# The sample tile of a fused input projection in fp32 on four column groups, and the projection slices moved between two units

## The chip, the cores and the metric

The kernel runs on one core of a Trainium2 chip. The metric is the device time of one execution in microseconds (us), as the median of several runs. The engines are TensorE (PE; its weight loads are shown apart as PEld), VectorE (DVE), ScalarE (ACT), GpSimd (POOL) and SyncE (SP), which here only starts DMAs.

## What is computed

Two layers of a transformer step over 512 prompt tokens and 32 sample tokens of width 1024. Layer 0 (the even one) mixes four differential-attention heads with eight stick-breaking heads; layer 1 (the odd one, "fox") is forgetting attention with 16 heads. In both, normed tokens are first projected by one wide weight; after the attention come an output projection and a mixture of experts. Cut to what the change touches:

```
x = concat(x_prompt (512 rows), x_sample (32 rows))
h = rmsnorm(x) * (1 + scale) + shift            # scale, shift from adaLN, apart for prompt and sample
q, k, v = split(h @ w_in)                       # w_in: 1024 x 3072, in fp32
# prompt rows attend to prompt rows; sample rows attend to 256 cached rows and to the 32 sample rows
# k and v of all rows are outputs as well
```

## The kernel before

A layer's projection and attention run together, as a pipeline over eight **blocks** of weight columns (NB = 8). A block is 384 columns (BW): 128 each of q, k and v, so one differential head or two of the other heads. The tokens stand in five **tiles**: t = 0 to 3 are 128 prompt rows each, t = 4 (called NT) is the 32 sample rows. A **unit** u = 5 i + t is the attention of block i for query tile t.

For each block, `fuse_load` (SP) brings the raw fp32 weights into `fu_raw`, in two halves of four DMAs. `fuse_high` (ACT, L612) rounds them to the fast format fp32r, `fuse_low` (DVE, L618) makes the rest, in four pieces. The tokens h are held in the same way, transposed, as `hT` and `hT2`. A **product** is one tile by one block: eight **slices** (one for each 128 of the 1024 inputs), and a slice is three matmuls (L563, L564, L565) of 128 rows by 384 columns: high by high, high by low, low by high. It goes into bank 0 or 1, alternately. The sample's tile takes the same 24 matmuls, as 128 columns of `hT` are loaded from its first column on, and only 32 of the 128 result rows are kept. The results are copied to `fu_rows` by `fuse_rows_act` (ACT, even t, L661) and `fuse_rows_dve` (DVE, odd t, L668).

The order on each engine is written out by hand. On PE, in `even_pe` and `fox_pe`, unit u holds: the scores of unit u+1 (`first` or `scores`), the transposes of its own weights (`second` or `turn`), the values (`values`), and between them slices of the product that is six units ahead, n = u + 6. In units 0 to 3 these are slices 0 to 2 (or 4), then up to 6, then 6 and 7. In unit 4 PE also transposes q and k of the next block (`turn_q_k`, L676) and its late keys (`turn_rest`, L676); the slices stand there in pairs. Unit 3 of block i so holds the sample's product of block i+1, and unit 4 the first product of block i+2. Before unit 0 comes a **lead** (`lead_pe`): it transposes h (L526), makes all five products of block 0 and the first of block 1. In layer 1 the lead also has `gate_logits` (matmuls on `wf_r`), whose results pass through a chain on DVE and ACT (L1691 to L1599) to the first scores. Other work on PE between the units: `ada_matvec` (L326), a vector by 512 columns in fp32 on four groups of 32 array columns, and `ada_sum` (L332).

On ACT, `q_out` (L1560) and `late_out` (L1564, L1565) bring the transposes of unit 4 out; then ACT copies tile 0 (L661), takes the exponentials of unit 0 (L1539) and copies the transposed weights (L1550). On DVE, `maxima` (L1630) and `normed` (L1637, L1640) do their part; `k_out` is L1647, `mixed` is L1654. Layer 0 has the same with other lines (values L942 for stick-breaking). SP starts in layer 1, for each block, the stores of k and v (`store`), then `fuse_load` of the block two ahead, then adaLN loads.

## Time and profile before

| what | value |
|---|---|
| median of 3 runs | 1740.81 us (1735.86 to 1748.72) |
| the profiled execution | 1750.45 us, of which the span is 1748.7 us |
| PE busy | 1486.2 us, 85% of the span |
| DVE, ACT, POOL busy | 1032.4, 865.5, 489.7 us |
| mean granted TensorE clock | 0.924 of full speed |
| bytes read from HBM | 341.87 MB |

The span is the time between the first and the last instruction; the time of the execution has 1.75 us around it. Busy time of PE adds up matmuls that overlap in its pipeline, so what a matmul costs is read from the distance of starts, not from its own length.

### The profile page before, as it was taken

To read this page: it belongs to the slowest core of one execution; us is meant where nothing else is said; L and a number is where in the kernel's file an instruction comes from. 1 tells how busy PE (TensorE), PEld (TensorE's weight loads), DVE (VectorE), ACT (ScalarE), POOL (GpSimd) and SP (SyncE) were. 2 spreads that over 40 slices of the span, in tenths; PEclk is the share of its full clock that TensorE was granted. 3 is DMA by queue.
4 is the path that set the end of the run, shared out by engine and by line. 5 is a ranking of instruction groups with operands and counts; after the bars stand their busy time and mean duration, and the time that the engine had idled before them with its cause. 6 is when DMAs were issued, how large, how long until landed. Compare 5 with 4: busy or idle time off the path is not lost.

```text
span 1748.7 us, 22798 instructions
## 1 busy us (share of the span) xinstructions
PE 1486.2 (85%) x7979; PEld 1162.0 (66%) x7979; DVE 1032.4 (59%) x1345; ACT 865.5 (49%) x1512; POOL 489.7 (28%) x379
## 2 busy tenths in 40 slices
PE   3499999997947999999937899999889399999981
PEld 0387777764735777877727677777567277878770
DVE  0555442224446988988956443333363568888995
ACT  2233334445124777777733333333341267788772
POOL 1200111110104666656521000000001155656650
PEclk8699999998967999999968999999989599999995
DMA  8435553133044899989970333443420479999984
GB/s 279 147 120 180 187 170 104 68 124 106 1 195 154 337 351 356 369 342 354 357 249 12 98 104 104 129 136 114 155 75 36 167 263 344 367 367 364 335 314 170
DMA packets 148608, 358.62 MB, mean 205 GB/s; under 512 B 18660, under 2 KB 80868, under 8 KB 122420
## 3 DMA queue, kind: packets, MB, share of 16 engines
q1 hardware_dynamic: 136184, 333.25, 52.7%
q0 software_dynamic: 12352, 24.40, 3.8%
q8 instruction: 45, 0.74, 0.2%
q14 instruction: 27, 0.22, 0.0%
HBM read 341.87 MB, written 33.56 MB: 215 GB/s over the span
## 4 chain that ended last, share of the span: by engine, by line
PE 65%; DVE 12%; issue 7%; ACT 6%; DMA 5%; SPq 2%; DVEq 1%; POOL 0%; POOLq 0%; ACTq 0%; PEldq 0%; PEld 0%
PE bank L563 17%; PE bank L565 15%; PE bank L564 15%; DVE ring_r L1945 4%; DMA ring<-in_w_gate 2%; PE bank L326 2%; ACT work_r L1938 2%; PE bank L1447 2%; PE bank L1485 1%; PE bank L676 1%; PE bank L332 1%; PE bank L1462 1%; PE bank L2231 1%; PE bank L919 1%; PE bank L558 1%
## 5 line engine op out<-in xcount | busy, mean ns | idle before, releaser
L564 PE MATMUL bank<-ring_r,arena_r 128*128 128x512 f32 x816 | 323.6, 397 | 0.0
L563 PE MATMUL bank<-ring_r,hT_r 128*128 128x384 f32 x640 | 239.9, 375 | 1.6 <-ACT hT_r L494 1.6
L564 PE MATMUL bank<-ring_r,hT_r 128*128 128x384 f32 x640 | 217.0, 339 | 0.0
L565 PE MATMUL bank<-ring_r,work_r 128*128 128x384 f32 x640 | 217.0, 339 | 0.0
L1945 DVE TENSOR_TENSOR ring_r<-ring,work_r 128x1024 fp32r<-128x1024 f32 x102 | 177.2, 1763 | 28.2 <-ACT work_r L1938 28.2
L1945 DVE TENSOR_TENSOR ring_r<-ring,arena_r 128x1024 fp32r<-128x1024 f32 x96 | 166.4, 1771 | 29.3 <-ACT arena_r L1938 29.3
L564 PEld LDWEIGHTS bank<-ring_r,arena_r 128*128 128x128 f32 x816 | 157.3, 193 | 31.1
L1945 DVE TENSOR_TENSOR ring_r<-ring,hT_r 128x1024 fp32r<-128x1024 f32 x108 | 155.1, 1464 | 25.1 <-ACT hT_r L1938 24.3
L1938 ACT ACTIVATE hT_r<-ring 128x1024 fp32r<-128x1024 f32 x144 | 144.3, 1054 | 47.3 <-DMA ring<-in_w_gate 41.5
L563 PEld LDWEIGHTS bank<-ring_r,hT_r 128*128 128x128 f32 x640 | 121.7, 190 | 43.0 <-issue 39.1
L1938 ACT ACTIVATE work_r<-ring 128x1024 fp32r<-128x1024 f32 x136 | 136.6, 1059 | 6.9 <-DMA ring<-in_w_up 6.8
L1938 ACT ACTIVATE arena_r<-ring 128x1024 fp32r<-128x1024 f32 x128 | 126.8, 1052 | 21.6 <-DMA ring<-in_w_down 21.3
L1889 POOL TENSOR_TENSOR arena<-arena,bc 128x1024 f32<-128x1024 f32 (+1 forms) x6 | 14.3, 2382 | 434.9 <-DVE arena L1875 434.9
L563 PE MATMUL bank<-hT_r,arena_r 128*128 128x512 f32 x288 | 123.2, 428 | 8.9 <-DVE arena_r L2386 5.6
L564 PEld LDWEIGHTS bank<-ring_r,hT_r 128*128 128x128 f32 x640 | 122.2, 191 | 1.2 <-issue 0.7
L565 PEld LDWEIGHTS bank<-ring_r,work_r 128*128 128x128 f32 x640 | 121.3, 190 | 0.0
L565 PE MATMUL bank<-hT_r,arena_r 128*128 128x512 f32 x288 | 118.4, 411 | 0.0
L2421 POOL TENSOR_TENSOR ring_r<-ring,arena_r 128x1024 fp32r<-128x1024 f32 x32 | 86.3, 2696 | 90.9 <-ACT arena_r L1938 90.9
L563 PE MATMUL bank<-work_r,arena_r 128*128 128x512 f32 x272 | 109.2, 402 | 0.0
L2421 POOL TENSOR_TENSOR ring_r<-ring,hT_r 128x1024 fp32r<-128x1024 f32 x36 | 92.4, 2566 | 54.0 <-ACT hT_r L1938 40.4
L563 PE MATMUL bank<-arena_r 128*128 128x512 f32 x256 | 100.9, 394 | 6.7 <-DVE ring_r L1945 6.6
L565 PE MATMUL bank<-work_r,arena_r 128*128 128x512 f32 x272 | 106.4, 391 | 0.0
(356 smaller groups left out, 2880.3 us busy)
## 6 DMA issues: line engine op xcount, KB each, us to landing
ring<-in_w_gate SPq DMA_DIRECT2D x68, 1024.0 KB, 6.8
ring<-in_w_up SPq DMA_DIRECT2D x68, 1024.0 KB, 7.4
ring<-in_w_down SPq DMA_DIRECT2D x68, 1024.0 KB, 7.5
bc<-in_w_ada SPq DMA_DIRECT2D x40, 1024.0 KB, 6.8
bc<-in_w_in_even SPq DMA_DIRECT2D x64, 192.0 KB, 4.0
bc<-in_w_in_odd SPq DMA_DIRECT2D x64, 192.0 KB, 3.6
ring<-in_w_ada SPq DMA_DIRECT2D x4, 2048.0 KB, 12.3
arena<-moe_out SPq DMA_DIRECT2D x8, 1024.0 KB
```

The source lines that it names most:

```text
L326: last = nc.tensor.matmul(acc[32 * q:32 * q + 32, :], silu_c[:, 4 * h + q, :], ada_w[h][:, q, :], start=h == 0, stop=h == 1)
L332: nc.tensor.matmul(acc[0:32, :], pick[:, :], ada_part(pre), start=True, stop=True).then_inc(AD["sum"], 1)
L558: last = nc.tensor.matmul(acc, wr[:, k, :], hT[:, k, cols(t)], start=k == 0, stop=k == KD - 1)
L563: nc.tensor.matmul(acc, rows_hi, w_hi, start=first, stop=False)
L564: nc.tensor.matmul(acc, rows_hi, w_lo, start=False, stop=False)
L565: return nc.tensor.matmul(acc, rows_lo, w_hi, start=False, stop=last)
L676: last = nc.tensor.transpose(out_bank[0:np_, c:c + r], src, ident[0:r, 0:r])
L919: last = nc.tensor.matmul(b[:, 0:n], neg_from[:, :], s[:, 0:n], start=False, stop=True, skip_group_check=True)
L1447: nc.tensor.matmul(fx_bank(u, h)[0:r, 0:n], fx_qT[i % 2][half, cols(t)], fx_kT[i % 2][half, k0:k0 + n], start=True, stop=False)
L1938: act.activation(r32(piece(m_high[v], q)), piece(m_low[v], q), ACT.Copy).then_inc(MO[f"hi_{c}"], 1)
L1945: dve.tensor_tensor(r32(piece(m_low[v], q)), piece(m_low[v], q), f32(piece(m_high[v], q)), ALU.subtract).then_inc(MO[f"lo_{c}"], 1)
L2421: pool.tensor_tensor(r32(piece(m_low[v], 1)), piece(m_low[v], 1), f32(piece(m_high[v], 1)), ALU.subtract).then_inc(MO[f"lop_{c}"], 1)
```

## The change

1. The sample's product is no longer 24 fp32r matmuls. DVE copies the sample's transposed rows once for each layer into `sample_T` (`row_sample`), in plain fp32. `fuse_sample` multiplies them with the raw weights of a block: for each of eight slices four matmuls, one for each group of 32 array columns, which take 96 (SW) of the 384 weight columns each. That is 32 matmuls in fp32, each issued as two. ACT copies the result out in four pieces (`sample_rows`).
2. The order on PE. In the blocks, the sample's product is that of block i+2 (before: i+1), all of it in unit 3 between the scores and the transposes; the second stretch of slices in unit 3 is now slices 0 to 3 of the first product of block i+2, and unit 4 keeps slices 4 to 7 of it (1, 2 and 1). In the lead, the sample of block 0 comes ahead of tile 0, into bank 6, and that of block 1 behind tile 3. `gate_logits` in layer 1 is ahead of tile 3 (before: behind it).
3. Waits: `fuse_load` of block b also waits for the sample's product of block b-1, which reads `fu_raw`. The lead waits for `sample_T`. A product into the bank of the sample waits for the four copies. The stores of k and v wait for `ev_s` in place of the third ACT copy.
4. In layer 1's lead on DVE, the copy of tile 3 is later (behind all of `fuse_low` of block 1) and `k_out(0)` is moved from ahead of the chain of the gate to behind it.
5. The matrix `upto` (one memset and one select on POOL in the setup) is gone.

```diff
+        def row_sample(dve, l):
+            s, o = NORM, 2 * l
+            for half in range(2):
+                dve.wait_ge(s["ev_a"], EV_A[o] + half + 1)
+                dve.tensor_copy(sample_T[:, 4 * half:4 * half + 4, :], row_turned(0, half)).then_inc(s["smp"], 1)
...
             row_turn(pe, l, 0)
             row_turn(pe, l, 1)
+            pe.wait_ge(NORM["smp"], 2 * l + 2)
             row_turn(pe, l, 2)
-            for t in range(TILES):
-                row_evicted(pe, l, min(t + 1, TILES - 1))
-                if t == NT:
-                    pe.wait_ge(NORM["pad"], 2 * l + 2)
-                    if last_logits:
-                        last_logits()
+            fuse_sample(pe, l, 0, bank[6], 0, KD)
+            for t in range(NT):
+                row_evicted(pe, l, t + 1)
+                if t == NT - 1 and last_logits:
+                    last_logits()
                 fuse_product(pe, l, t, 0, KD)
                 if t + 3 < TILES:
                     row_turn(pe, l, t + 3)
+            fuse_product(pe, l, NT, 0, KD)
...
             if b >= 1:
                 sp.wait_ge(FU["lo"], 4 * g_b)
+                sp.wait_ge(FU["smp"], g_b)
...
+            b, t = n // TILES, n % TILES
+            if b + t // NT >= NB:
                 return
-            b, t = n // TILES, n % TILES
+            if k0 == 0 and n >= 2:
+                fuse_rows_out(pe, l, n - 2)
+            if t == NT:
+                fuse_sample(pe, l, b + 1, bank[n % 2], k0, k1)
+                return
...
+        def fuse_sample(pe, l, b, acc, k0, k1):
+
+            w = by_row(fu_raw)
+            for k in range(k0, k1):
+                if k % 4 == 0:
+                    pe.wait_ge(FU[f"raw{k // 4}"], 64 * (NB * l + b) + 64)
+                for q in range(4):
+                    last = nc.tensor.matmul(acc[DEC * q:DEC * (q + 1), 0:SW], sample_T[:, k, :], w[:, k, SW * q:SW * (q + 1)],
+                                            start=k == 0, stop=k == KD - 1)
+            if k1 == KD:
+                last.then_inc(FU["smp"], 1)
...
+        def sample_rows(act, l, b, acc):
+
+            act.wait_ge(FU["smp"], NB * l + b + 1)
+            fuse_rows_free(act, l, b)
+            for q in range(4):
+                act.activation(fu_rows[b % 2][0:DEC, NT, SW * q:SW * (q + 1)], acc[DEC * q:DEC * (q + 1), 0:SW],
+                               ACT.Copy).then_inc(FU["ev_s"], 1)
...
                 if t == NT:
-                    fuse_product(pe, 1, n, 0, 2)
                     if i + 1 < NB:
                         turn_q_k(i + 1)
                     turn(u)
-                    fuse_product(pe, 1, n, 2, 4)
+                    fuse_product(pe, 1, n, 4, 5)
                     if i + 1 < NB:
                         turn_rest(i + 1)
-                    fuse_product(pe, 1, n, 4, 6)
+                    fuse_product(pe, 1, n, 5, 7)
                     values(u)
                     if i + 1 < NB:
                         scores(u + 1)
-                    fuse_product(pe, 1, n, 6, KD)
+                    fuse_product(pe, 1, n, 7, KD)
                 else:
                     scores(u + 1)
                     k = 4 if t == 0 else 2
-                    fuse_product(pe, 1, n, 0, k)
+                    if t == NT - 1:
+                        fuse_product(pe, 1, n, 0, KD)
+                    else:
+                        fuse_product(pe, 1, n, 0, k)
                     turn(u)
...
-                    fuse_product(pe, 1, n, k, 6)
+                    if t == NT - 1:
+                        fuse_product(pe, 1, n + 1, 0, 4)
+                    else:
+                        fuse_product(pe, 1, n, k, 6)
                     values(u)
...
-                    fuse_product(pe, 1, n, 6, KD)
+                    if t < NT - 1:
+                        fuse_product(pe, 1, n, 6, KD)
...
+                if t == 0 and 1 <= i < NB - 1:
+                    sample_rows(act, 1, i + 1, sample_bank(i + 1))
                 fuse_rows_act(act, 1, u + TILES)
...
-            k_out(0)
+            fuse_rows_dve(dve, 1, 3)
             dve.wait_ge(FG["act"], FG_ACT["log"])
...
             dve.drain().then_inc(FG["dve"], 1)
+            k_out(0)
             maxima(0)
```

PE in units 3 and 4 of a block of layer 1, before (L1447, L1451 and L1453 are the scores, L1462 the transposes, L1485 the values, L676 `turn_q_k` and `turn_rest`; of each stretch of slices the last row stands):

```order
L1447 MATMUL bank<-arena 32x288 x2
...
L565 MATMUL bank<-ring_r,work_r 128x384
L1462 MATMUL bank<-ident,arena 128x128 x8
...
L565 MATMUL bank<-ring_r,work_r 128x384
L1485 MATMUL bank<-arena 64x128 x8
...
L565 MATMUL bank<-ring_r,work_r 128x384
L676 MATMUL bank<-ident,arena 128x128 x8
L1462 MATMUL bank<-ident,arena 128x32 x2
```

The same place after the change (the lines are those of the changed kernel: L1496 the scores, L1511 the transposes, L1534 the values, L717 `turn_q_k`, L652 the sample, L569 the third matmul of a slice):

```order
L1496 MATMUL bank<-arena 32x288 x2
L1500 MATMUL bank<-d_b,sel_b 32x288 x2
L1502 MATMUL bank<-causal_b,ident_b 32x32 x2
L652 MATMUL bank<-bc,sample_T 32x96 x32
L1511 MATMUL bank<-ident,arena 128x128 x8
...
L569 MATMUL bank<-ring_r,work_r 128x384
L1534 MATMUL bank<-arena 64x128 x8
L717 MATMUL bank<-ident,arena 128x128 x8
L1511 MATMUL bank<-ident,arena 128x32 x2
```

The stretch of slices behind the scores has become the 32 matmuls of the sample, and none stands any longer between the values of unit 3 and `turn_q_k`.

ACT between unit 4 of one block of layer 1 and unit 0 of the next, before:

```order
L1564 ACTIVATE arena<-bank 128x288
L1565 ACTIVATE arena<-bank 128x32
L661 ACTIVATE arena<-bank 128x384
L1539 ACTIVATE arena,small<-bank,small 128x128 x2
L612 ACTIVATE ring_r<-bc 128x768
```

and after:

```order
L1619 ACTIVATE arena<-bank 128x288
L1620 ACTIVATE arena<-bank 128x32
L679 ACTIVATE arena<-bank 32x96 x4
L699 ACTIVATE arena<-bank 128x384
L1594 ACTIVATE arena,small<-bank,small 128x128 x2
L618 ACTIVATE ring_r<-bc 128x768
```

The sample's four copies stand ahead of the copy of tile 0 and of the exponentials of unit 0; before, one copy of 32x384 (L661) stood ahead of `q_out`.

DVE in layer 1's lead, around the chain of the gate, before:

```order
L668 COPY arena<-bank 128x384
L1683 TENSOR_SCALAR arena<-bank,bf_t 16x512
L1684 TENSOR_SCALAR arena<-bank,bf_t 16x32
L1686 COPY arena<-bank 16x256
L618 TENSOR_TENSOR ring_r<-bc,ring_r 128x768 x2
L1647 COPY arena<-bank 128x512
L1691 SCALAR_TENSOR_TENSOR arena<-arena 16x544
```

and after:

```order
L1741 TENSOR_SCALAR arena<-bank,bf_t 16x512
L1742 TENSOR_SCALAR arena<-bank,bf_t 16x32
L1744 COPY arena<-bank 16x256
L624 TENSOR_TENSOR ring_r<-bc,ring_r 128x768 x2
L706 COPY arena<-bank 128x384
L1749 SCALAR_TENSOR_TENSOR arena<-arena 16x544
```

The copy of tile 3 now stands ahead of L1749 (before: L1691), and `k_out(0)` (L1647) no longer does.

## Rows read from the trace of the kernel before

**Rows 1.** Windows of one block each, layers 0 and 1: us, busy times, clock, DMA

```profile
148.60:186.92 38.32, 38.32 (x239) 29.09 (x243) 19.56 (x53) 13.65 (x39) 4.08 (x6) 1.00 0.52 174
281.07:325.49 44.42, 44.37 (x266) 32.70 (x270) 12.08 (x21) 20.71 (x54) 7.32 (x11) 1.00 0.32 103
1072.40:1111.36 38.96, 38.96 (x273) 29.99 (x276) 15.07 (x35) 14.77 (x43) 0.00 (x0) 1.00 0.36 113
```

**Rows 2.** Timeline of PE, units 3 and 4 in layer 1: start, us

```profile
1084.15 0.45 PE L563 MATMUL bank<-ring_r,hT_r 128*128 128x384 f32 x1
...
1085.32 1.04 PE L1462 MATMUL bank<-ident,arena 128*128 128x128 f32 x8
...
1087.26 0.45 PE L563 MATMUL bank<-ring_r,hT_r 128*128 128x384 f32 x1
...
1089.56 1.09 PE L1485 MATMUL bank<-arena 128*64 128x128 f32 x16
1090.58 0.44 PE L563 MATMUL bank<-ring_r,hT_r 128*128 128x384 f32 x1
...
1092.80 1.03 PE L676 MATMUL bank<-ident,arena 128*128 128x128 f32 x8
...
1097.13 0.66 PE L1485 MATMUL bank<-arena 128*64 128x32 f32 x12
...
1099.57 0.70 PE L1447 MATMUL bank<-arena 64*128 64x256 f32 x4
...
1102.70 0.38 PE L1462 MATMUL bank<-ident,arena 128*128 128x128 f32 x2
```

**Rows 3.** Timeline of PEld and PE at one matvec on four column groups

```profile
1072.33 0.16 PEld L326 LDWEIGHTS bank<-bc,silu_c 128*32 128x32 f32 x8 [0.17 <-issue]
1072.79 0.13 PEld L326 LDWEIGHTS bank<-bc,silu_c 128*32 128x32 f32 x4 [0.30 <-issue]
1073.22 0.13 PEld L326 LDWEIGHTS bank<-bc,silu_c 128*32 128x32 f32 x4 [0.30 <-issue]
...
1072.33 1.92 PE L326 MATMUL bank<-bc,silu_c 128*32 128x512 f32 x16
```

**Rows 4.** Timelines of ACT and DVE around unit 0 of that block

```profile
1096.29 0.19 ACT L1565 ACTIVATE arena<-bank 128x32 f32<-128x32 f32 x1
1099.68 0.49 ACT L661 ACTIVATE arena<-bank 128x384 f32<-128x384 f32 x1 [3.19 <-PE bank L565]
...
1101.10 0.48 DVE L1640 TENSOR_SCALAR arena<-arena,small 128x128 f32<-128x128 f32 x2
```

**Rows 5.** Raw weights of layer 1: page part 6 (us to landing), timelines of SP and ACT

```profile
bc<-in_w_in_odd SPq DMA_DIRECT2D x64, 192.0 KB, 3.6
...
948.68 3.03 ACT L612 ACTIVATE ring_r<-bc 128x768 fp32r<-128x768 f32 x4
...
1094.44 4.15 SPq L603 DMA_DIRECT2D bc<-in_w_in_odd  x8
...
1100.75 0.85 ACT L612 ACTIVATE ring_r<-bc 128x768 fp32r<-128x768 f32 x1
```

**Rows 6.** Timeline of PE, lead of layer 0

```profile
71.66 1.97 PE L526 MATMUL bank<-ident,arena 128*128 128x128 f32 x8 [1.65 <-POOL arena L511]
75.24 0.66 PE L563 MATMUL bank<-ring_r,hT_r 128*128 128x384 f32 x1 [1.62 <-ACT hT_r L494]
76.34 0.52 PE L563 MATMUL bank<-ring_r,hT_r 128*128 128x384 f32 x1
```

**Rows 7.** Timelines of DVE and PE, lead of layer 1

```profile
923.20 0.48 DVE L500 TENSOR_TENSOR work_r<-bank,hT_r 128x128 fp32r<-128x128 f32 x2
948.09 0.34 PE L563 MATMUL bank<-ring_r,hT_r 128*128 128x384 f32 x1
952.28 0.40 PE L563 MATMUL bank<-hT_r,wf_r 128*128 128x512 f32 x1
960.56 0.42 PE L563 MATMUL bank<-ring_r,hT_r 128*128 128x384 f32 x1
967.56 0.70 DVE L1691 SCALAR_TENSOR_TENSOR arena<-arena 16x544 f32<-16x544 f32 x1
975.29 0.49 PE L1447 MATMUL bank<-arena 64*128 64x128 f32 x4 [4.21 <-ACT logf L1599]
```

**Rows 8.** Timeline of PE, unit 3 of block 7 in layers 0 and 1

```profile
412.73 1.08 PE L942 MATMUL bank<-arena 128*64 128x512 f32 x4 [0.69 <-ACT arena L1076]
1274.53 1.09 PE L1485 MATMUL bank<-arena 128*64 128x128 f32 x16 [0.85 <-ACT arena L1550]
```

More of the change, by code:

```diff
@@ L224, in setup_pool @@
             pool.affine_select(out=strict_b[:, :], in_=strict_b[:, :], compare_op=ALU.is_ge, fill=NEG, base=-1,
-                               pattern=[[1, P]], channel_multiplier=-1)
-            pool.affine_select(out=upto[:, :], in_=upto[:, :], compare_op=ALU.is_ge, fill=0.0, base=0,
                                pattern=[[1, P]], channel_multiplier=-1)
@@ L429, in encoder_step @@
         junk = arena[:, 14336:15360]
-        NORM = sems("norm", "square", "rstd", "scaled", "shifted", "tr", "ev_a", "ev_v", "self", "gain", "shift_v", "pad")
+        NORM = sems("norm", "square", "rstd", "scaled", "shifted", "tr", "ev_a", "ev_v", "self", "gain", "shift_v", "smp")
         NORM_NO = {"norm_mix0": 0, "norm_ffn0": 1, "norm_mix1": 2, "norm_ffn1": 3}
@@ L628, in fuse_product @@
                     pe.wait_ge(FU["lo"], 4 * (NB * l + b) + k // 2 + 1)
-                if k == 0 and n >= 2:
-                    fuse_rows_out(pe, l, n - 2)
                 last = split_product(bank[n % 2][:, 0:BW], tile_cols(hT_flat, k, t), tile_cols(hT2_flat, k, t),
@@ L657, in fuse_rows_act, with sample_bank @@
             b, t = n // TILES, n % TILES
-            if n < NB * TILES and t % 2 == 0:
-                act.wait_ge(FU["mm"], UNITS * l + n + 1)
+            if n < NB * TILES and t in (0, 2):
+                act.wait_ge(FU["mm"], NT * (NB * l + b) + t + 1)
                 fuse_rows_free(act, l, b)
-                act.activation(fu_rows[b % 2][0:rows(t), t, :], bank[n % 2][0:rows(t), 0:BW], ACT.Copy).then_inc(FU["ev_a"], 1)
+                act.activation(fu_rows[b % 2][:, t, :], bank[n % 2][:, 0:BW], ACT.Copy).then_inc(FU["ev_a"], 1)
         def fuse_rows_dve(dve, l, n):
             b, t = n // TILES, n % TILES
-            if n < NB * TILES and t % 2 == 1:
-                dve.wait_ge(FU["mm"], UNITS * l + n + 1)
+            if n < NB * TILES and t in (1, 3):
+                dve.wait_ge(FU["mm"], NT * (NB * l + b) + t + 1)
                 fuse_rows_free(dve, l, b)
-                dve.tensor_copy(fu_rows[b % 2][0:rows(t), t, :], bank[n % 2][0:rows(t), 0:BW]).then_inc(FU["ev_v"], 1)
+                dve.tensor_copy(fu_rows[b % 2][:, t, :], bank[n % 2][:, 0:BW]).then_inc(FU["ev_v"], 1)
+        def sample_bank(b):
+            return bank[6] if b == 0 else bank[(TILES * b - 1) % 2]
         def fx_bank(u, h):
@@ L1601, in fox_act @@
                 i, t = u // TILES, u % TILES
+                if t == 0 and 1 <= i < NB - 1:
+                    sample_rows(act, 1, i + 1, sample_bank(i + 1))
                 fuse_rows_act(act, 1, u + TILES)
```

78 lines of the change are left out of this document (46 added, 32 removed).

## The prediction

> **What bounds the kernel now.** I read the windows of single blocks first, then the timeline of PE inside one, then what ACT, DVE and SP do beside it. In the blocks of both layers PE is busy for the whole window at clock 1.00, while DVE and ACT are busy for half of it or less [rows 1]. The reader is to see that a block lasts as long as its PE instructions do: what leaves PE there leaves the time, as long as no other engine's chain then ends later. This holds for blocks 0 to 5; in block 7, which has no product beside it, PE waits for ACT and DVE [rows 8], and in the leads it waits for the rows of h [rows 6] and for the gate's chain [rows 7].
>
> **Price of a slice.** Eight slices in a row take 948.09 to 952.28, 4.19 us, so 0.524 us a slice [rows 7]. A short stretch costs more, as PE changes between kinds of matmul: two slices 1084.15 to 1085.32, 1.17 us; four 1087.26 to 1089.56, 2.30 us; the last two of unit 3 with the first two of unit 4 1090.58 to 1092.80, 2.22 us [rows 2]. So each change costs 0.1 to 0.2 us.
>
> **Part 1, the slices that go.** Units 3 and 4 held 16 slices. The 1.17 us behind the scores go, the 2.22 us behind the values of unit 3 go, and of the three pairs left in unit 4 two slices go, 2 x 0.524 = 1.05 us. The four slices at 1087.26 stay, as slices of another product. Sum: 4.44 us of PE in each block.
>
> **Part 2, the sample in fp32.** 32 matmuls, each issued twice, so 64 instructions on four column groups. The trace has this kind with 512 columns: PEld loads weights in groups of four, 1072.79 and 1073.22, so a round of four instructions takes 0.43 us, and all 16 fit into 1.92 us [rows 3]. 96 columns are 96/512 of it: 0.081 us a round, 16 rounds 1.29 us, and 0.25 us for the changes of kind at both ends. I take 1.55 us. The lower bound is 1.29 us. The upper bound comes from the densest short matmuls of the trace, twelve with 32 columns and 64-column weights in 0.66 us [rows 2], of which about 0.22 us is the length of the last: 0.44/11 = 0.04 us an instruction, 64 x 0.04 + 0.25 = 2.8 us. I stay near the lower end because those twelve load twice as many weight columns, and the matvec has the same weights (128x32), the same four groups and the same loop.
>
> **A steady block** so loses 4.44 - 1.55 = 2.9 us. There are six in each layer: 12 x 2.9 = 34.8 us.
>
> **What hides the rest in the steady blocks.** The four copies on ACT stand ahead of the copy of tile 0. ACT is free from the end of L1565, 1096.48, to 1099.68 [rows 4], 3.2 us; a copy is at most the 0.49 us of the 128x384 one, four are at most 1.96 us. The sample's product for them is long done. Slices ahead of that tile-0 copy are one fewer, so copy, exponentials and the transposes that wait for them all come 0.52 us earlier together: the weights are ready at 1101.58 and PE asks at 1102.70 [rows 2, 4], a margin of 1.1 us that stays. In unit 4 the cover is four slices instead of eight, but `turn_q_k` (1.03 us), `turn_rest` and three of the four slices still stand between a transpose and the values that need it, over 2 us for an ACT copy of about 0.5. Bank 0 or 1 is asked for earlier by the first product in unit 3; DVE copies tile 3 out at the start of that unit. The new wait of `fuse_load` ends with the sample's product, early in unit 3, about when `fuse_low` ends, for which it waits anyway. On SP the stores are ahead of it in the queue; they no longer wait for the sample's copy in unit 4, so both should start up to 8 us earlier than 1094.44, for weights that ACT takes at 1100.75 [rows 5]. I cost all of this at nothing; without the cover it is the stall below.
>
> **Layer 0's lead.** It loses the sample's 4.19 us and gains 1.55 us for block 1's. Block 0's sample falls into the 1.62 us in which PE waits for hT [rows 6]. The first slice there takes 1.10 us (75.24 to 76.34), twice 0.524, so the clock is at its lower level, 1.2 GHz, and the sample may last 2.6 us; but what it does slowly the tile behind it then does less slowly. With DVE's two more copies I take 0.2 us. Net 2.4 us.
>
> **Layer 1's lead.** Tile 2 ends at 948.09 [rows 7]; ahead of it come the sample, 1.55 us, and DVE's two copies, below the 0.48 us of the like pair L500, say 0.4. So tile 2 ends near 950.0, the logits (952.28 to 960.56, 8.28 us) near 958.3, tile 3 near 962.5, its copy near 963.2. There the gate's chain starts, which started at 967.56, as `k_out` is out of its way; the first scores come 7.73 us behind that start, so near 970.9 instead of 975.29. PE itself arrived at 971.08 (4.21 us before the scores); it loses 4.19 us and gains twice 1.55 and 0.4: 970.4, and the transposes of the gate's rows still have to pass ACT. I take 971.2, a gain of 4.1 us. The load of block 1 must now wait for block 0's sample, near 936; 4.15 us of issue and 3.6 us to landing make 943.8, and ACT takes it at 948.68 or later [rows 5]. Everything behind the first scores moves with them.
>
> **Block 6.** Its unit 3 held the sample of block 7, now one block earlier: about 1.17 + 2.30 + 1.2 = 4.7 us go with nothing in their place. Bare, the same unit waits 0.69 us in layer 0 and 0.85 us in layer 1 [rows 8]; with the next wait, and a clock that may fall sooner, I take 3.2 us in each layer, between 2.2 and 4.0: 6.4 us.
>
> The setup's two POOL instructions less: nothing, as the setup is not ended by POOL's last select.
>
> **Sum.** 34.8 + 2.4 + 4.1 + 6.4 = 47.7 us. The profiled execution of 1750.45 us would become 1702.8 us. It is 0.6% above the median; against the median of 1740.81 us the same gain gives 1693 us. With 1.44 to 2.1 us for a sample, block 6's bounds and a median that moves by some 6 us (the runs span 1735.86 to 1748.72), this case reaches from 1683 to 1704 us.
>
> **Rivals.**
>
> *Issue-bound sample.* The sample's 128 PE instructions (64 loads, 64 matmuls) have only 0.02 us for each pair. No row shows PE keep that up for 64 of them: the matvec has 16. At the upper bound of 2.8 us each of the 16 samples costs 1.25 us more, 20 us: 1713 us. For it: the count. Against it: in the matvec eight loads start within 0.16 us [rows 3]. The Trainium skill, TensorE: Matmul & The Clock Gate, section "Wait — 56ns, not 53.3ns?", says that starts of matmuls are never closer than about 25 ns, and that the sequencer may spend about 62 ns on each. Sixteen matmuls of about 0.6 us within 1.92 us do not show the first broken or kept; by the second, as an estimate from that page, a sample would take 4.2 us and the kernel 1736 us. By 25 ns it would be 1.85 us and 1698 us, inside my range.
>
> *A stall in the thinned unit.* With four slices fewer in unit 4 one wait ends last: the exponentials of unit 0 behind ACT's four copies. It decides once those copies end over 1.1 us late, against a free stretch of 3.2 us. At 1.5 us for each of 12 blocks, 18 us: 1711 us.
>
> *The column groups run one after another (slower).* Then a sample is 64 x 0.081 + 0.25 = 5.4 us, 3.9 us more than taken, 62 us in all: 14 us above before, 1755 us. It decides where a round of four passes (4.44 - 0.25)/16 = 0.26 us in place of 0.081; from there a steady block gains nothing. Against it stands the matvec: sixteen of its instructions, one after another, would take 6.9 us and took 1.92.
>
> **How the numbers follow.** Forecast 0.68; issue-bound 0.16; stall 0.10; serial groups 0.03; a gain beyond the range 0.03. The predicted time is 1693 us. From 1682 to 1714 us takes in the forecast, and both rivals at their price, and leaves out what lies beyond them. About 1% is what a measurement of this kernel can tell from no change; below 1723 us counts as faster: 0.94. Within 1%, by the serial groups or an issue rate near the slow end: 0.045. Slower by over 1%: 0.015.
>
> **What the changed profile would show.** Blocks 35.4 to 36.1 us apart in layer 1 (38.96 before) and PE still busy throughout; the group of L652 with 64 starts within 1.3 to 1.6 us; no wait of PE longer than 0.3 us in units 3, 4 and 0 of blocks 1 to 5; the first scores of layer 1 some 4 us sooner, with PE's wait ahead of them below 1 us; raw weights issued in unit 3. The forecast is wrong if the sample's stretch passes 2.1 us, if PE waits for ACT ahead of unit 0's transposes, or if ACT's L618 waits for a DMA in the blocks.

## The result, and the profile after

| | median of runs | ratio to before, 95% interval |
|---|---|---|
| before | 1741.49 us (1735.86 to 1748.72, 4 runs) | |
| changed | 1691.21 us (1689.09 to 1696.15, 4 runs) | 0.971 (0.9683 to 0.9737) |

That is 50.3 us less (predicted: 1693 us, 47.7 us less). The profiled execution took 1689.62 us, its span is 1687.9 us, 60.8 us less than the span before. PE's busy time went from 1486.2 to 1431.1 us and is still 85% of the span.

First the windows of one block each, in the order and with the columns of [rows 1]:

```profile
141.52:177.01 35.49, 35.49 (x276) 26.34 (x275) 19.38 (x54) 14.12 (x42) 4.07 (x6) 1.00 0.57 188
266.69:308.22 41.53, 41.49 (x304) 29.93 (x303) 11.98 (x21) 21.18 (x57) 7.28 (x11) 1.00 0.35 109
1035.16:1071.27 36.11, 35.95 (x309) 27.07 (x309) 15.06 (x35) 15.24 (x46) 0.00 (x0) 1.00 0.41 126
```

The columns are the window, its length, the busy time and count of PE, PEld, DVE, ACT and POOL, PE's granted clock, the DMA share and GB/s. The blocks are 2.83, 2.89 and 2.85 us shorter, and PE is still busy for all of them (but for 0.16 us in layer 1) at full clock. The window lost what PE lost, and DVE, the next busiest, is busy for 55% at most.

The timeline of PE in units 3 and 4 of one block of layer 1, which answers to [rows 2]:

```profile
1046.98 1.53 PE L652 MATMUL bank<-bc,sample_T 128*32 128x96 f32 x64
1048.44 1.09 PE L1511 MATMUL bank<-ident,arena 128*128 128x128 f32 x8
1049.46 1.04 PE L329 MATMUL bank<-bc,pick 128*32 128x512 f32 x2
1050.44 0.44 PE L567 MATMUL bank<-ring_r,hT_r 128*128 128x384 f32 x1
...
1052.74 1.09 PE L1534 MATMUL bank<-arena 128*64 128x128 f32 x16
1053.76 1.09 PE L717 MATMUL bank<-ident,arena 128*128 128x128 f32 x8
```

The sample's whole product is the first line: 64 starts, and the transposes begin 1.46 us behind its first (1.55 predicted). The four moved slices stand from 1050.44 to 1052.74, 2.30 us, as the slices in this place did before. No line in this stretch has idle time in brackets.

The lead of layer 1 answers to [rows 7]. Its first transposes before, then the timeline of PE after; L1496 here is the first scores, L1534 the first values:

```profile
918.62 1.03 PE L526 MATMUL bank<-ident,arena 32*128 32x32 f32 x8 [27.52 <-POOL arena L511]
```

```profile
890.12 1.03 PE L529 MATMUL bank<-ident,arena 32*128 32x32 f32 x8 [27.51 <-POOL arena L514]
902.94 1.94 PE L529 MATMUL bank<-ident,arena 128*128 128x128 f32 x8 [6.14 <-issue]
904.81 2.75 PE L652 MATMUL bank<-bc,sample_T 128*32 128x96 f32 x64
907.50 0.44 PE L567 MATMUL bank<-ring_r,hT_r 128*128 128x384 f32 x1
...
942.89 0.49 PE L1496 MATMUL bank<-arena 64*128 64x128 f32 x4 [0.49 <-issue]
...
953.37 0.70 PE L1534 MATMUL bank<-arena 128*64 128x128 f32 x4 [5.16 <-ACT arena L1605]
```

From the first transpose to the first scores it is 52.77 us; before it was 56.67 (918.62 to 975.29, the latter in [rows 7]). The wait ahead of the scores was 4.21 us and is 0.49 us. The sample of block 0 runs here at the lower clock level (granted 0.50; 2.75 us in place of 1.53).

By stages, from the starts of the adaLN matvecs, which both kernels have at the same places: up to the last matvec of layer 0, 23.3 us less (406.08 and 382.79); layer 1 from its first transposes to its first matvec 3.0 less (75.81 and 72.83); its six steady blocks 17.1 less (233.72 and 216.64); its block 6 4.8 less (32.44 and 27.66). That is 48.1 us (the terms are rounded). The other 12.7 us between the two profiles lie in the two stages of experts with the output projections, where the kernels do not differ: 512.5 against 507.3 us in layer 0, 488.1 against 480.6 in layer 1. In the profile of e4, which has the old code there as well, these took 506.4 and 491.2 us. So they vary by some us from execution to execution, and the medians, 50.3 us apart, agree with the 48.1 of the stages.

### The profile page after: what moved, and what is told of

Its sections match the earlier page's. It is cut to its first block, busy times and chain, and to the rows that moved or that the text cites. A ratio compares the mean times of both kernels' runs of the same rounds, so it can differ in the third digit from the quotient of the medians.

```text
span 1687.9 us, 24152 instructions
## 1 busy us (share of the span) xinstructions
PE 1431.1 (85%) x8611; PEld 1110.8 (66%) x8619; DVE 1010.1 (60%) x1349; ACT 874.6 (52%) x1560; POOL 495.2 (29%) x377
## 4 chain that ended last, share of the span: by engine, by line
PE 65%; DVE 10%; DMA 8%; issue 6%; ACT 6%; SPq 2%; DVEq 1%; POOLq 0%; ACTq 0%; PEldq 0%; POOL 0%; PEld 0%
PE bank L567 15%; PE bank L569 14%; PE bank L568 14%; DMA ring<-in_w_gate 4%; DVE ring_r L2004 3%; PE bank L323 2%; DMA ring<-in_w_down 2%; PE bank L1496 2%; PE bank L1534 2%; ACT work_r L1997 1%; PE bank L652 1%; PE bank L717 1%; PE bank L1511 1%; PE bank L329 1%; PE bank L959 1%
## 5 line engine op out<-in xcount | busy, mean ns | idle before, releaser
L2004 DVE TENSOR_TENSOR ring_r<-ring,work_r 128x1024 fp32r<-128x1024 f32 x102 | 173.5, 1726 | 33.1 <-ACT work_r L1997 33.0
L567 PE MATMUL bank<-ring_r,hT_r 128*128 128x384 f32 x512 | 191.8, 375 | 0.0
L2004 DVE TENSOR_TENSOR ring_r<-ring,arena_r 128x1024 fp32r<-128x1024 f32 x96 | 157.6, 1676 | 30.6 <-ACT arena_r L1997 30.6
L569 PE MATMUL bank<-ring_r,work_r 128*128 128x384 f32 x512 | 172.8, 337 | 0.0
L568 PE MATMUL bank<-ring_r,hT_r 128*128 128x384 f32 x512 | 172.7, 337 | 0.0
L2004 DVE TENSOR_TENSOR ring_r<-ring,hT_r 128x1024 fp32r<-128x1024 f32 x108 | 144.9, 1369 | 27.0 <-ACT hT_r L1997 25.6
L567 PE MATMUL bank<-hT_r,arena_r 128*128 128x512 f32 x288 | 121.3, 421 | 10.3 <-DVE arena_r L2445 7.1
L569 PE MATMUL bank<-hT_r,arena_r 128*128 128x512 f32 x288 | 117.1, 406 | 0.0
L567 PEld LDWEIGHTS bank<-ring_r,hT_r 128*128 128x128 f32 x512 | 96.6, 189 | 30.2 <-issue 28.1
L2480 POOL TENSOR_TENSOR ring_r<-ring,arena_r 128x1024 fp32r<-128x1024 f32 x32 | 90.7, 2836 | 82.2 <-ACT arena_r L1997 82.2
L569 PE MATMUL bank<-work_r,arena_r 128*128 128x512 f32 x272 | 106.4, 391 | 0.0
L567 PE MATMUL bank<-arena_r 128*128 128x512 f32 x256 | 100.7, 394 | 4.5 <-DVE ring_r L2004 4.0
L569 PE MATMUL bank<-arena_r 128*128 128x512 f32 x256 | 99.8, 390 | 0.0
L568 PEld LDWEIGHTS bank<-ring_r,hT_r 128*128 128x128 f32 x512 | 97.0, 190 | 1.1 <-issue 0.7
```

The lines of the kernel that those rows point to most:

```text
L567: nc.tensor.matmul(acc, rows_hi, w_hi, start=first, stop=False)
L568: nc.tensor.matmul(acc, rows_hi, w_lo, start=False, stop=False)
L569: return nc.tensor.matmul(acc, rows_lo, w_hi, start=False, stop=last)
L2004: dve.tensor_tensor(r32(piece(m_low[v], q)), piece(m_low[v], q), f32(piece(m_high[v], q)), ALU.subtract).then_inc(MO[f"lo_{c}"], 1)
L2480: pool.tensor_tensor(r32(piece(m_low[v], 1)), piece(m_low[v], 1), f32(piece(m_high[v], 1)), ALU.subtract).then_inc(MO[f"lop_{c}"], 1)
```

## The experiments

The medians come from several sessions, in which that of the kernel before lay between 1738.98 and 1743.82 us; each ratio is to the kernel before in the same session (it is not exactly the quotient of the two medians), so runs of different sessions are better compared by it. The blocks are distances of matvecs in each run's profile; "lead" is from the first transposes of layer 1 to its first scores.

| run | median us | ratio, 95% interval | block, layer 0 | block, layer 1 | lead |
|---|---|---|---|---|---|
| changed | 1691.21 | 0.971 (0.9683 to 0.9737) | 35.49 | 36.11 | 52.77 |
| e8, the same | 1692.44 | 0.9714 (0.9688 to 0.974) | 35.48 | 36.11 | 52.88 |
| e1, one group | 1754.11 | 1.0075 (1.0043 to 1.0106) | 39.33 | 39.93 | 59.79 |
| e2, two groups | 1713.87 | 0.9814 (0.9759 to 0.9868) | 36.77 | 37.37 | 54.87 |
| e5, half the columns | 1688.92 | 0.9679 (0.9653 to 0.9706) | 34.89 | 35.47 | 51.62 |
| e4, move only | 1744.33 | 0.9998 (0.9964 to 1.0033) | 38.29 | 38.90 | 56.26 |
| e3, no move | 1697.93 | 0.9716 (0.966 to 0.9773) | 36.49 | 35.95 | 52.33 |
| e10, no move, sample split | 1698.25 | 0.9744 (0.9702 to 0.9785) | 35.91 | 35.95 | 52.69 |
| e6, gate late | 1693.36 | 0.9715 (0.9693 to 0.9738) | 35.49 | 36.11 | 56.47 |
| e7, early load | 1686.36 | 0.9693 (0.9669 to 0.9716) | 35.48 | 36.11 | 52.33 |
| e11, the same | 1681.63 | 0.9657 (0.9629 to 0.9684) | 35.49 | 36.11 | 52.99 |
| e9, early load, layer 1 not moved | 1683.84 | 0.9671 (0.9636 to 0.9706) | 35.49 | 35.95 | 53.31 |

### What sets the length of the sample: e1, e2, e5

```diff
-                for q in range(4):
-                    last = nc.tensor.matmul(acc[DEC * q:DEC * (q + 1), 0:SW], sample_T[:, k, :], w[:, k, SW * q:SW * (q + 1)], ...)
+                last = nc.tensor.matmul(acc[0:DEC, 0:BW], sample_T[:, k, :], w[:, k, :], ...)                      # e1
+                for q in range(2): ... acc[DEC * q:DEC * (q + 1), 0:2 * SW] ... w[:, k, 2 * SW * q:2 * SW * (q + 1)]  # e2
+                for q in range(4): ... acc[DEC * q:DEC * (q + 1), 0:SW // 2] ... w[:, k, SW * q:SW * q + SW // 2]     # e5
```

Not shown: in e1 and e2 the four copies on ACT read the results from where they now lie; in e5 they repeat the 48 columns, so that half of the sample's q, k and v is left out.

e1: 

> The changed kernel, with the sample's product of a slice as one fp32 matmul of 32x384 in place of four of 32x96 in four column groups; positions, copies and the moved slices stay. Theory (the four groups run beside each other, a round of four taking 82 ns because 96 columns flow by): one group needs four times as long for each of 16 records, 0.33 us, so a sample takes some 5.3 us + 0.25 in place of 1.5. Twelve samples in steady blocks at +3.9 us give +47, the four in the leads +8 to +16: about 1750 us (1740 to 1757), no better than the kernel before, and the steady block of layer 1 is about 40 us long. Rival (the 82 ns are what it takes to hand over four instructions, 20 ns each, and not the flow of columns): one wide matmul for four narrow ones takes at most half of that, a sample 2.6 us or less, and the time stays under 1712. Rival (the gain came from the moved slices and not from the sample): less than 5 us of change.

e2: 

> The changed kernel, with the sample's product of a slice in two column groups of 192 columns each. If the groups run beside each other and the time is that of the columns of one group, a round takes 0.165 us and a sample 2.65 + 0.2, which is +1.3 us on each of twelve steady blocks and on the leads: 1691 + 16 to 21 = about 1709. If the hand-over of instructions sets it, two instructions for four make the sample no longer than now and the time stays within 5 us of 1691. If only the change of kind at the ends cost something, the same.

e5: 

> The changed kernel, with only 48 of the 96 columns in each of the sample's matmuls (the other half of the sample's q, k and v is left out and repeats the first half), all counts of instructions as they are. Theory (the round of four takes what 96 columns take to flow by, 82 ns): a round takes 41 ns and a sample 0.66 + 0.2, -0.65 us on each of 16 samples: 1691 - 8 to 11 = about 1681. Rival (the queue hands over no more than an instruction per 20 ns): the round stays at 80 ns or so and the time within 3 us of 1691. Between: a round of 62 ns gives -0.3 us each, 1686.

The sample's stretch in one block of layer 1, from the timelines of PE, of e1:

```profile
1061.48 5.35 PE L651 MATMUL bank<-bc,sample_T 128*32 128x384 f32 x16
```

of e2:

```profile
1066.29 2.79 PE L652 MATMUL bank<-bc,sample_T 128*32 128x192 f32 x32
```

and of e5:

```profile
1040.02 0.89 PE L652 MATMUL bank<-bc,sample_T 128*32 128x48 f32 x64
```

The work of e1, e2 and the changed kernel is the same; only on how many column groups it lies differs. The stretch is 5.35, 2.79 and 1.53 us, so it nearly halves with each doubling of the groups: they run beside each other. The single starts in the trace of the changed kernel show it directly: the four matmuls of a round start 6 or 7 ns apart, and the next round 62 or 63 ns behind the last of them (87 at first), some 82 ns behind the first. The differences, over 16 rounds, are 0.160 us for 192 columns more, 0.079 for 96 and, with e5, 0.040 for 48. So a round takes 0.83 ns for each column of one group, down to 48 columns. The rival that the hand-over of instructions is what takes 20 ns each fell with e1 (5.35 us and not 2.6) and again with e5 (64 instructions, 0.89 us and not 1.5).

The blocks follow: 35.47, 36.11, 37.37 and 39.93 us differ by 0.64, 1.26 and 2.56 us, and so do the four stretches. What PE has less the block has less, one for one, and in e1 all of the gain and 12.6 us more are gone. The prediction's slower rival had 5.4 us for a sample and 1755 us in all; e1, built to be that case, has 5.35 and 1754.11 us. The stretch and the blocks are the evidence; that the totals agree within 1 us is chance, as e1's ten runs lie between 1746.60 and 1766.65 us. e2 took 1713.87 us where 1709 was expected: sixteen samples at 1.26 us more make 20 us, and the other 2 to 3 us lie within the spread of its four runs (1710.28 to 1718.40). e5 took 2 us less than the changed kernel and not 10. Its blocks did what was expected, but the last stage of its profile, from the last matvec on, took 490.3 us against 480.6. e5 hands other values to the experts; whether that or the variation of this stage (e4 had 491.2) is the cause is not shown.

### What the move is worth: e4, e3, e10

e4 is the kernel before with the move alone; e3 is the changed kernel without it. For layer 1 (layer 0 has the same), e4:

```diff
                 if t == NT:
-                    fuse_product(pe, 1, n, 0, 2)
                     ...
-                    fuse_product(pe, 1, n, 2, 4)
+                    fuse_product(pe, 1, n, 4, 5)
                     ...
-                    fuse_product(pe, 1, n, 4, 6)
+                    fuse_product(pe, 1, n, 5, 7)
                     ...
-                    fuse_product(pe, 1, n, 6, KD)
+                    fuse_product(pe, 1, n, 7, KD)
                 else:
                     ...
-                    fuse_product(pe, 1, n, 0, k)
+                    if t == NT - 1:
+                        fuse_product(pe, 1, n, 0, KD)
+                    else:
+                        fuse_product(pe, 1, n, 0, k)
                     turn(u)
                     ...
-                    fuse_product(pe, 1, n, k, 6)
+                    if t == NT - 1:
+                        fuse_product(pe, 1, n + 1, 0, 4)
+                    else:
+                        fuse_product(pe, 1, n, k, 6)
                     ...
-                    fuse_product(pe, 1, n, 6, KD)
+                    if t < NT - 1:
+                        fuse_product(pe, 1, n, 6, KD)
```

> The kernel before (sample in the split fp32r product, 24 matmuls of 32x384), with only the second half of the change: the whole product of the sample ahead of the turn of unit 3, slices 0 to 3 of the next block's tile 0 behind it, and 4, 5-6, 7 in the sample's unit. Theory (the move alone brings nothing, it only fills the place that the sample left): 1741 with -5 to +6, since PE is busy throughout and the sum of its work stays. Rival (the move is worth half of the gain, because the sample's unit was where PE waited): 1705 to 1725. Rival (the sample ahead of the turn now delays the softmax of unit 4 by 5 us of work): 1750 to 1765.

e3 undoes the same lines in the changed kernel, so that unit 3 has nothing of a product between `turn` and `values`:

> The changed kernel, but slices 0 to 3 of the next block's tile 0 stay in the sample's unit (0-1 ahead of the turns of q and k, 2-3 and 4-5 behind the turns, 6-7 behind the scores), so that nothing of the product lies between the turn and the values of unit 3. Theory of the prediction (matmuls between turn and values cover ScalarE's copy of the turned weights): the values of unit 3 wait for that copy, 1 to 2.3 us longer than now less what the sample's unit saves, +0.4 to +1.5 us for each of 13 blocks: 1696 to 1710. Rival (PE has enough slack behind it, another engine waits anyway): within 3 us of 1691. Rival (the fuller sample's unit was itself short of cover): faster than 1688.

e10 is e3 with half of the sample behind the turn. Against e3, in layer 0 (layer 1 has the same):

```diff
                     if t == NT - 1:
-                        fuse_product(pe, 0, n, 0, KD)
+                        fuse_product(pe, 0, n, 0, 4)
                     else:
                         fuse_product(pe, 0, n, 0, k)
                     second(u)
                     ...
                     if t < NT - 1:
                         fuse_product(pe, 0, n, k, 6)
+                    else:
+                        fuse_product(pe, 0, n, 4, KD)
                     values(u)
```

> The kernel of e3 (slices 0 to 3 not moved), but slices 4 to 7 of the sample's product behind the turn of unit 3 in place of ahead of it: 0.66 us of matmuls between the turn and the values, which in layer 0 followed each other directly. In e3 TensorE waits 0.69 us there in each block of layer 0 for ScalarE's copy of the turned weights, and not in layer 1, where the sum of the adaLN row (1.0 us) stands between. Theory (the moved slices are worth just this cover): the wait of layer 0 goes, its block goes from 36.49 to 35.7 to 35.9, layer 1's stays within 0.15 of 35.95, and the time is e3's less 3 to 4.5: 1694. Rival (the move is worth a us because of the order in the sample's unit): the blocks stay at 36.4 and the time at 1698.

By itself the move is worth nothing that the time shows (e4: ratio 0.9998; the blocks in the table are 0.05 us shorter or less, the two last steady ones of layer 0 0.25 us). With the short sample it is worth 1.0 us a block in layer 0 (0.8 in those two) and costs 0.16 us in layer 1. The whole time does not tell e3 and the changed kernel apart: their medians are 6.7 us apart, but the ratios are 0.9716 and 0.971. The timeline of PE of e3 shows the greater part of the difference in the blocks, first unit 3 in layer 0, then in layer 1:

```profile
200.41 1.16 PE L926 MATMUL bank<-arena 128*128 128x128 f32 x8 [0.69 <-ACT arena L1086]
201.50 1.04 PE L329 MATMUL bank<-bc,pick 128*32 128x512 f32 x2
...
1051.35 1.09 PE L1510 MATMUL bank<-ident,arena 128*128 128x128 f32 x8
1052.37 1.04 PE L329 MATMUL bank<-bc,pick 128*32 128x512 f32 x2
1053.35 1.09 PE L1533 MATMUL bank<-arena 128*64 128x128 f32 x16
```

The values must wait for ACT's copy of the transposed weights. In layer 1 `ada_sum` (L329) stands between the transposes and the values and covers the copy; in layer 0 it stands behind the values, and PE waits 0.69 us. In e10 no such wait is left, and the block of layer 0 comes to 35.91 us, at the upper end of what was expected:

```profile
200.14 0.66 PE L903 MATMUL bank<-ident,arena 128*128 128x128 f32 x4
200.73 0.87 PE L652 MATMUL bank<-bc,sample_T 128*32 128x96 f32 x32
201.57 1.16 PE L926 MATMUL bank<-arena 128*128 128x128 f32 x8
```

I had expected the loss of e3 in both layers, and had overlooked `ada_sum`. The wait is 0.69 us of the 1.0; the other 0.3 to 0.4 us in layer 0 (35.91 against 35.49 in e10, with no wait) and the 0.16 us of layer 1 go with the other division of the slices, and no run takes that apart. e10's median did not follow its blocks (1698.25 us, expected 1694). Its four runs lie between 1688.58 and 1704.10 us and cannot show 4 us; in its profile layer 0 lost 2.7 us of the gain again in the last block pair (34.2 us against 31.6 in e3's), see below.

### The lead of layer 1: e6, e7, e11, e9

e6 puts the logits back where they were:

```diff
-                if t == NT - 1 and last_logits:
-                    last_logits()
                 fuse_product(pe, l, t, 0, KD)
                 ...
+            if last_logits:
+                last_logits()
             fuse_product(pe, l, NT, 0, KD)
```

> The changed kernel, with the gate's logits of layer 1's lead behind the product of tile 3, as in the kernel before, in place of ahead of it; nothing else moved. Theory of the prediction (the chain of the gate sets the first scores of layer 1, and with the logits ahead of tile 3 its 5.1 us lie beside it): the chain starts 5.1 us later, the matmuls that then stand behind it (1.5 of the sample, 2.3 of slices, the turns) no longer cover it, PE waits 3 to 5 us ahead of the gate's transposes, and the time is 1691 + 3.5 to 5 = about 1695. Rival (the saving of the lead is the sample's alone, 3 us of product for 1.5): within 1.5 us of 1691.

The lead is 56.47 us, 3.7 more than in the changed kernel and as long as before. So with the logits late all but 0.2 us of the 3.9 us is lost again, and the sample's shorter product by itself brings next to nothing here. The size is as expected (3 to 5 us), but the wait is not where I expected it: ahead of the first scores PE waits 0.41 us in e6, as in the changed kernel, and not for the gate's chain. A row of DVE in e6, then PE's timeline:

```profile
938.44 0.54 DVE L706 COPY arena<-bank 128x384 f32<-128x384 f32 x1
...
939.03 0.44 PE L567 MATMUL bank<-ring_r,hT_r 128*128 128x384 f32 x1 [1.95 <-DVE arena L706]
939.31 0.47 PE L568 MATMUL bank<-ring_r,hT_r 128*128 128x384 f32 x1
939.58 0.52 PE L569 MATMUL bank<-ring_r,work_r 128*128 128x384 f32 x1
```

The next product needs the bank of tile 3, whose copy on DVE (L706) now stands behind the logits' own work there. That is 1.95 us; the other 1.7 us are the clock. Behind the wait the starts are 0.27 to 0.32 us apart and not 0.17, and the granted clock from 939.10 to 942.00 is 0.55. e6 keeps the changed order on DVE, so it is not the lead of before. There the chain's first step (L1691, 967.56) stood behind `k_out`, which waited for PE:

```profile
966.95 0.69 DVE L1647 COPY arena<-bank 128x512 f32<-128x512 f32 x1 [3.27 <-PE bank L676]
```

In e6 `k_out` is out of the chain's way, and the wait of 4.21 us for the chain stays away even with late logits. So the new order on DVE is what removes that wait, at least in e6, and it is also what makes late logits costly. Neither was tried without the other: no run has `k_out` at its old place. 3.7 us are 0.2% of the whole; the median (+2.2 us against the changed kernel, +0.9 against e8) can't show it apart from chance, the profile can.

e7 moves a load on SP's queue:

```diff
             past(1)
+            fuse_load(sp, 1, 2)
             sp.wait_ge(FG["act"], FG_ACT["rows"])
             ...                                    # two stores of the gate
             for i in range(NB):
                 store(i)
-                if i + 2 < NB:
+                if 1 <= i < NB - 2:
                     fuse_load(sp, 1, i + 2)
```

> The changed kernel, with the load of block 2's raw weights of layer 1 issued ahead of the two stores of the gate and the four of block 0's rows on SP's queue, so that it waits only for block 1's last low part and sample product (936 us in the profile after) and not for the gate's last copy (942.7). In the profile after ScalarE waits 6.4 us for this transfer and the first values of layer 1 wait 5.2 us for ScalarE. Theory: the load is issued some 9.5 us sooner, both waits go, and the time is 1691 - 4 to 5 = about 1686.5. Rival (the next thing is late by as much: the first two tiles' softmax, or the stores that now start 4 us later hold up the rows' copies): within 1.5 us of 1691.

In the changed kernel (timelines of SP, then of ACT):

```profile
943.92 0.37 SPq L1413 DMA_DIRECT2D out_fox_k_p<-arena  x1
...
945.96 4.09 SPq L609 DMA_DIRECT2D bc<-in_w_in_odd  x8
...
951.23 0.84 ACT L618 ACTIVATE ring_r<-bc 128x768 fp32r<-128x768 f32 x1 [6.41 <-DMA bc<-in_w_in_odd]
...
952.88 0.44 ACT L1605 ACTIVATE arena<-bank 128x128 f32<-128x128 f32 x2
```

ACT waits in order for the raw weights of block 2, and the copy that PE's first values need (L1605) stands behind that wait: the 5.16 us of PE. The windows of PE behind it (us, busy, clock, DMA share, GB/s):

```profile
948.00:953.30 5.30, 0.21 (x2) 0.86 1.05 303
953.30:958.50 5.20, 5.13 (x17) 0.50 0.97 364
958.50:963.00 4.50, 4.50 (x37) 0.99 0.01 2
```

The wait is paid twice: behind it the granted clock is at its lower level (0.50, 1.2 GHz) for about 5 us. In e7 the load is issued at 928.62, and there is neither:

```profile
936.80:948.00 11.20, 11.20 (x76) 1.00 0.74 239
```

From the first scores to the first matvec it is 12.5 us in e7 (935.30 to 947.8) and 20.1 in the changed kernel, 7.6 us less: 5.2 of wait, 2.4 of clock. I had expected the wait alone.

e11 and e9 stood beside each other. e9 is e7 with the slices of layer 1 as in e3:

> The kernel of e7 once more, beside e9: 1686 within 3, and 64.8 us from the first transposes of layer 1 to its first matvec, as in e7 (72.9 in the changed kernel). Of its 8.1 us, 5.2 are the wait and 2.4 the clock, which in the profile after stood at its lower level (0.50) for some 5 us behind the wait and doubled the slices there. If the rest of e7's lower profiled time (1674.8 against 1689.6) belonged to the run, this profile shows it in the stages of experts again with other amounts.

> The kernel of e7 (early load of block 2's raw weights in layer 1), and in layer 1 alone slices 0 to 3 of the next block's tile 0 back in the sample's unit as in e3; layer 0 keeps the moved slices. In e3's profile a steady block of layer 1 takes 35.95 us and not 36.11, in layer 0 36.49 and not 35.49: if that comes from the block itself, this kernel's profile shows 35.5 in layer 0 and 35.95 in layer 1, 8 us less than the changed kernel between the first transposes of layer 1 and its first matvec, and the time is 1.0 us below e7's (6 x 0.16), 1685. Rival (35.95 against 36.11 was chance of the one profile): equal to e7. Rival (the shorter lead moves the blocks against the transfers): above e7 by 1 us or more.

e11 has no wait in this place either, and again 12.5 us from scores to matvec, where the changed kernel and e8 have 20.1 and 20.3. The ten runs of e7 and e11 have a median of 1684.95 us, the ten of the changed kernel and e8 1691.5, 6.6 us apart, close to the 7.6 of the profiles. e7 alone is not clear of e8, which ran beside it (the intervals overlap); e11 is. So the early load beats both kernels. e9's blocks are 35.49 and 35.95 us, as expected, but its median is 2.2 us above e11's and its interval overlaps: the 1.0 us of the six blocks is not to be seen in the time.

e8 was run for the noise:

> The changed kernel as it is, once more beside these three, to see what of a difference of a few us belongs to the run: 1691, within 3. In its profile the steady blocks keep their 35.5, 41.5 and 36.1 us within 0.1, while the stages of experts, which no kernel here touches, vary by some us between profiled executions (324.6 us in the profile before and 317.7 in the one after for the first of the two), if their difference was the transfers' and not the change's.

Its blocks in the table are the changed kernel's to 0.01 us, and its stages of experts are near (506.6 us in layer 0 against 507.3, 481.8 against 480.6 in layer 1); e7's profile had 501.3 us in layer 0. Its last block pair of layer 0 took 31.55 us and not 33.15, and its first matvec stood 2.2 us later. So one profile of a kernel gives these stages to some 2 us, and those of the experts to more.

## Why the prediction held, by its steps

**The price of a slice, part 1 and part 2.** The sample has 1.46 us to the next start, 1.55 was taken; the rate of 96/512 of the matvec's round was right, as e1, e2 and e5 show over a factor of eight. A steady block of layer 1 lost 2.85 us, 2.9 was taken, so the slices that went were 4.31 us and not 4.44. In layer 0 the six blocks gave 15.9 us in these profiles where 17.4 was taken, see the next step.

**The cover.** Blocks 1 to 5 of layer 1 have no wait of PE but 0.16 us of issue, and ACT's L618 waits for no transfer in them. SP issues the stores from 1046.62 on and the weights at 1048.77, in unit 3, as predicted. One miss, against the sign of no wait over 0.3 us: in layer 0, between 228.24 and 266.69, PE waits 0.99 us at L717 for an adaLN row whose bias lands late, and that block gives 1.7 us and not 2.9. It varies with the execution: e8, the same kernel, waits 0.2 us there and e7 not at all, and e7's matvecs are 37.5 us apart, 2.6 less than before.

**Layer 0's lead.** 2.4 us taken, 4.2 in the profiles (first matvec 110.20 and 106.03). But 1.0 us of that is a setup that ended sooner: the transposes that wait for POOL start at 71.66 before [rows 6] and at 70.62 after. From them to the first matvec it is 38.54 and 35.41 us, 3.1 less. The seven other profiles with this lead have 35.7 to 36.3 us, and e4, with the lead of before, has 39.94. So 2.4 is the right size, and these profiles can't say it closer than 2 to 4.5. The rows, to compare with [rows 6]:

```profile
72.49 2.50 PE L652 MATMUL bank<-bc,sample_T 128*32 128x96 f32 x64
74.92 0.44 PE L567 MATMUL bank<-ring_r,hT_r 128*128 128x384 f32 x1
```

Here the clock rose during the sample (at 74.55), and the slices of tile 0 are at full clock from the first, where before the first eight matmuls or so were at half. In e8 it rose at 77.41, within the tile. Counted from the transposes tile 0 ends 9.20 us behind them before, 8.59 here and 9.08 in e8. So the step, that the slowness of the sample and of the tile cancel, held within 0.6 us.

**Layer 1's lead.** The first scores came 3.9 us sooner, 4.1 taken. The wait on the gate's chain went, as named (4.21 us, now 0.49 and for something else). PE's own way to the scores is as long as before (52.28 and 52.46 us from the first transposes without these waits), where 0.7 us less was taken. The prediction named both causes, the earlier logits and `k_out`; how they share the gain is open (e6). But "everything behind the first scores moves with them" was wrong. The first values wait for a copy behind a transfer, 3.5 us before and 5.2 after, and the lead to the first matvec gave 3.0 us. These are the rows before:

```profile
983.49 0.84 ACT L612 ACTIVATE ring_r<-bc 128x768 fp32r<-128x768 f32 x1 [6.24 <-DMA bc<-in_w_in_odd]
...
985.63 0.44 PE L1485 MATMUL bank<-arena 128*64 128x128 f32 x4 [3.49 <-ACT arena L1550]
```

The transfer's issue sits behind the stores, 3.0 us behind the first scores before and 3.1 after (978.24 and 945.96), and the first values follow the first scores by 10.3 and 10.5 us, though PE is busy for 1.5 us less between them (behind the wait of 4.21 us before, its clock was low there, 0.64 up to 980.00, and is 1.00 now): that gain turned into wait. The rest of the lost 0.9 us lies behind the wait, where the clock stayed low for longer (mean 0.81 from the values to the matvec before, 0.73 after). I had not followed these rows.

**Block 6.** 3.2 us taken in each layer, 4.0 at most; 3.2 and 4.8 in the profiles. PE's clock in these windows was 0.93 before and 1.00 after in layer 1. The window of the changed kernel, then of e7 and of e11, which are one kernel run twice:

```profile
1179.59:1207.25 27.66, 22.74 (x180) 1.00 0.56 194
...
1164.41:1192.08 27.67, 22.90 (x181) 1.00 0.56 193
...
1169.67:1199.16 29.49, 25.18 (x180) 0.88 0.59 208
```

So some 1.8 us of this term is whether the clock falls in the short waits there, and the kernel does not decide that. In layer 0 the clock fell in the changed kernel's profile (33.15 us at 0.95) and not in e8's (31.55 us at 1.00), where the term is 4.8 us as well. The prediction allowed for a clock that falls and not for one that stays up, so the term was taken too small.

**Rivals.** The issue-bound sample is refuted by the sample's 1.53 us and by e5, the serial groups by e1 and e2; e1 shows that the second had the price of a kernel without overlap right. The first could have been weighed down beforehand. The prediction says that the matvec's sixteen matmuls leave open whether starts can be closer than 25 ns, which is a wrong reading of the merged row in [rows 3]: singly, in the trace before, the four of a round start at 1072.787, 1072.794, 1072.800 and 1072.807, 6 or 7 ns apart. The stall in the thinned unit did not come; e3 shows a stall of that kind, 0.69 us, in unit 3 of layer 0, when the moved slices are taken out.

**Sum.** 34.8 + 2.4 + 4.1 + 6.4 was forecast; the stages give 19.1 (layer 0 behind its lead, of which 3.2 is block 6) + 4.2 + 3.0 + 17.1 + 4.8 = 48.1 us before rounding. Against the forecast that is -1.5 (blocks of layer 0), +1.8, -1.1, -0.3 and +1.6 us (block 6). The errors have both signs and cancel to 0.4 us. That is luck, as e8's profile, of the same kernel, has other errors in the lead and block 6 of layer 0. The main term, twelve steady blocks, is right by its mechanism (33.0 us of 34.8).

## What to carry to other kernels

A tile of 32 rows that is multiplied as if it had 128 throws three quarters of the result rows away. With its rows as the stationary side, and the columns of the other split over four groups, even plain fp32 (1.53 us) is faster than three fp32r products of full width (4.19 us); on one group it is slower (5.35 us). It also takes the weights as they come, without rounding. Three fp32r products on four groups were not tried. A move of work on a saturated engine was worth mainly the wait that it covers: ask for each place what already stands between a step and its reader. And look at what a wait does to the clock behind it; here a wait of 5.2 us cost 7.6.

## What the runs showed of the hardware

In e5 64 matmuls of 48 columns on four groups started within 0.68 us (0.89 less the 0.206 us that the last one lasts), 10.8 ns apart on average: three steps of 6 or 7 ns from group to group, then one of 22 or 23 ns (47 at first) to the next round. As many weight loads stand between them in the trace. The Trainium skill, TensorE: Matmul & The Clock Gate, section "Wait — 56ns, not 53.3ns?", says that starts of matmuls are never closer than about 25 ns. The measurement differs: for matmuls on different column groups that limit does not hold. The 62 ns for each matmul that the same section gives for the sequencer did not show either; by them, as an estimate, the sample would have taken 4 us.

For one group, e1's starts are 0.32 us apart for 384 columns, twice 384 cycles of 2.4 GHz, where the fp32r matmuls of 384 columns start 0.17 to 0.18 us apart. So each of the two instructions of an fp32 matmul passes its columns at half the rate.
